# Moving the hand-placed SBUF area so that matmul operands and the weight ring start at the same place modulo 2048 bytes

## The chip, the cores and the metric

The program runs on one core of one Trainium2 chip. The metric is the device time of one execution in microseconds; lower is better. Three runs of the kernel before took 3888.85, 3893.64 and 3898.47 us, median 3893.64 us.

## What is computed

A stack of three transformer layers over one sequence of 512 tokens of width 1024, all in float32:

```python
for i in range(2):                                    # first block
    h = h + (mixer_ab if i == 0 else mixer_c)(rmsnorm(h))          # attention and recurrence
    h = h + conv_glu_ffn(rmsnorm(h))                               # 1024 -> 5632 -> 1024
    h = h + sigmoid(rmsnorm(h) @ ple_gate) * (p[i] @ ple_proj)
# second block: one layer
h = h + merged(diff_attention, chunk_attention)(rmsnorm(h)) @ w_out
h = h + peer(rmsnorm(h))     # routing picks 16 of 16384 single-neuron experts for each of 8 heads
return rmsnorm(h)
```

`peer` is computed densely: `gelu(xn @ u.T)` for all 16384 experts, times a routing matrix, times `v`. With the dense layers this makes one stream of 272 weight slots of 1 MB each.

## The kernel before

**Precision.** Every large product is made from operands that are split in two float32r parts, high and low. `split_product` (the matmul is line 189) issues three matmuls for one 128 x 128 x 512 product: high by high, low by high, high by low. Each is a weight load of 128 x 128 elements (512 bytes of each partition) and a stream of up to 512 moving columns (2048 bytes of each partition).

**The weight stream.** SyncE loads slot after slot (16 tiles of 128 x 128) into `weights_raw` (two places of 8 KB of each partition). GpSimd makes the high part with one TENSOR_SCALAR (line 2593) and the low part with one TENSOR_TENSOR (line 2595) in `weights_split`, the ring: two places of 16 KB, of which the first 8 KB are the high part and the next 8 KB the low part. TensorE waits for a place (`weights_ready`), uses it for 48 matmuls, and frees it for GpSimd. The hand-over, the order of the stages and all waits are written out by hand, and nothing in them depends on an address.

**Who is moving and who is loaded.** In most products a ring tile is loaded as weights and an operand of the hand-placed area moves (rows `banks<-memory,weights_split`). In the products "by token" and in the second half of the expert layer it is the other way round: 128-token slices of the operand are loaded and the ring moves (rows `banks<-weights_split,memory`).

**Where things lie.** In each partition, 16,512 bytes are taken by the runtime's scratch and four small constants; then come `residual` (16 KB, from byte 16,512), `weights_raw` (16 KB), `weights_split` (32 KB, from byte 49,280), `constants` (6,180 bytes, from 82,048), `columns` (2,912 bytes, from 88,256). The hand-placed area begins at the next multiple of 256, byte 91,392. Within it `Common` (line 498) takes 14 KB for four work tiles, `rstd` and the embedding, and two vectors of 128 bytes; then X_AT (32 KB), B_AT (56 KB) and HN_AT (32 KB) follow, in which every stage places its own buffers with `take` (line 235), rounded up to 128 bytes. Modulo 2048 this gives: residual, raw weights and ring tiles of index 0 at 128; the common tiles at 1280; the buffers that start at X_AT, B_AT and HN_AT at 1536. Modulo 256 the ring is at 128 and the area at 0. The tiles within a slot step by 512 bytes, the 512-column tiles of an operand by 2048.

**Lines that matter.** 189 split matmuls; 2593 and 2595 GpSimd's split; 443, 446 (ScalarE) and 452, 459 (VectorE) the norm's per-tile work, from `residual` into the area; 611 and 776 VectorE additions into `residual` and 677 one into a PSUM bank; 2213 a float32 matmul of one-hot rows and columns (`rows`, `cols`, both in the area, 512 bytes apart inside a tile and both tiles at the same place modulo 2048); 2240 float32 matmuls that load `residual` and move the identity of `constants`; 2361, 2367, 2483 the expert layer's gating; 2414 its activation; 2436 and 2439 the loads of routing and hidden values into the area; 1459 copies of 383 columns into rows that lie 1532 bytes apart.

Of the kernel before, what the change touches and what calls it, by code (L numbers as in the profile page):

```python
# [40 lines left out]
P = 128  # L41
TOKENS = 512
BLOCKS = TOKENS // P
# [41 lines left out]
CONST_AT, CONST_N = offsets(CONST_WIDTHS)  # L85
COLUMN_AT, COLUMN_N = offsets(COLUMN_WIDTHS)
# [90 lines left out]


KB = 1024
LINE = 128  # L180
X_AT = 14 * KB + 2 * LINE
B_AT = X_AT + 32 * KB
HN_AT = B_AT + 56 * KB


def split_product(k, out, left, right, start, stop):
# [9 lines left out]
class Core:  # L196


    def __init__(self, nc, ctx, dram):
        self.nc, self.ctx, self.dram = nc, ctx, dram  # L200
        self.period = None
        self.h = self.sbuf("residual", [P, D_TILES * TOKENS])
        self.raw = self.sbuf("weights_raw", [P, RING * SLOT])
        self.ring = ctx.enter_context(nc.sbuf_tensor("weights_split", [P, RING * 2 * SLOT], F32R))
        self.consts = self.sbuf("constants", [P, CONST_N])
        self.columns = self.sbuf("columns", [P, COLUMN_N])
        self.banks = ctx.enter_context(nc.psum_tensor("banks", [P, 8, 512], F32))
        self.arena = (nc.sbuf_base + 2 * LINE - 1) // (2 * LINE) * (2 * LINE)
        self.raw_in = [self.sem(f"weights_raw_in_{i}") for i in range(RING)]
        self.high_made = self.sem("weights_high_made")  # L210
        self.weights_ready = [self.sem(f"weights_split_{i}") for i in range(RING)]
        self.weights_used = [self.sem(f"weights_used_{i}") for i in range(RING)]
        self.meetings = self.sem("meetings")
        self.inputs_in = self.sem("inputs_in")
        self.held = self.sem("held")
        self.filled = self.sem("dense_filled")
        self.freed = {"vector": self.sem("dense_freed_vector"), "scalar": self.sem("dense_freed_scalar")}
        self.x_high, self.x_low, self.squared, self.summed, self.inverted = (
            self.sem(s) for s in ("operand_high", "operand_low", "squared", "squares_summed", "norm_inverted"))
        self.fills, self.frees, self.users, self.next_bank = 0, {"vector": 0, "scalar": 0}, {}, 0  # L220
        self.counts, self.kept = {}, {}
        self.tiles = 0
        self.pointer, self.named = 0, 0

    def sbuf(self, name, shape):
        return self.ctx.enter_context(self.nc.sbuf_tensor(name, shape, F32))
# [10 lines left out]
    def take(self, columns, dtype=F32):  # L237

        self.named += 1
        at = self.arena + self.pointer  # L240
        self.pointer += (4 * columns + LINE - 1) // LINE * LINE
        return self.nc.alloc_sbuf_tensor_at(f"memory_{self.named}", [P, columns], dtype, offset=at)[:, :]

    def take_split(self, tiles):
# [253 lines left out]
class Common:  # L498
# [3 lines left out]
    def __init__(self, k):  # L502
        self.work = [k.take(512) for _ in range(4)]
        self.rstd = k.take(512)
        self.embedding = k.take(PLE_TILES * 512)
        self.token_deviation, self.token_rstd = k.take(BLOCKS), k.take(BLOCKS)
        self.embedding_in = k.lasting("embedding_in")


# [654 lines left out]
def mixer_ab(k, common, hn, after_norm):  # L1164

    first = Norm(k, "mix0", hn, common, by_token=True)
    with k.scope(at=B_AT):
        heads = k.take(20 * 512)
        values = k.take(BLOCKS * 1024)
    with k.scope(at=X_AT):  # L1170
        out = k.take(BLOCKS * 1024)
    with k.scope(at=X_AT + 28 * KB):
        masks = k.take(8 * P)
# [6 lines left out]
    def evacuate(dve, n, bank):  # L1180
# [6 lines left out]
                           lambda part, b: cut(values, b * 1024 + part * 512, 512), meet=True)]  # L1187
    with k.scope(at=HN_AT):
        stages.append(stick_breaking(k, qa, ka, values, 1024, out, X_AT + 16 * KB))
    keep, decay = heads[:, 0:2048], heads[:, 2048:4096]  # L1190
# [300 lines left out]
def mixer_c(k, common, normed, after_norm):  # L1491
    with k.scope(at=B_AT):
# [3 lines left out]
        out = k.take(BLOCKS * 1024)  # L1496
    with k.scope(at=X_AT):
        table = k.take(SW_HEADS * 256)
# [114 lines left out]
def branches(k, common, normed, after_norm):  # L1613
# [22 lines left out]
        merged_high = k.take(8 * 512, F32R)  # L1636
    with k.scope(at=low_at):
        merged = Operand(k, merged_high, 8, k.take(8 * 512, F32R))
    with k.scope(at=HN_AT + 32 * KB):
        columns = Columns(k, 67)  # L1640
    even, odd = common.work[0:3], [common.work[3], odd_buffer]
    turned = [cut(common.embedding, n * 512, 512) for n in range(2)] + [third_turned]
# [876 lines left out]
def program(nc, dram):  # L2519
    ctx = ExitStack()  # L2520
    with ctx:
        k = Core(nc, ctx, dram)

        with k.scope(at=0):
            common = Common(k)
        assert k.arena + B_AT + 88 * KB <= nc.sbuf_usable_end
        with k.scope(at=X_AT):
            x = k.take(2 * D_TILES * TOKENS, F32R)
        with k.scope(at=HN_AT):
            hn = k.take(2 * D_TILES * TOKENS, F32R)  # L2530
        ffn_norm = [Norm(k, f"ffn{i}", x, common) for i in range(2)]
        ple_norm = [Norm(k, f"ple{i}", x, common) for i in range(2)]
        mix1_norm = Norm(k, "mix1", hn, common, by_token=True)
        norm1 = Norm(k, "norm1", hn, common, by_token=True)
        norm2 = Norm(k, "norm2", x, common)

        def layer(i):
            with k.scope(at=B_AT):
                stages = [load_embedding(k, i, common)] + feed_forward(k, i, common, ffn_norm[i], ple_norm[i])
            with k.scope(at=B_AT):  # L2540
                return stages + [layer_embedding(k, i, common, ple_norm[i], norm1 if i else mix1_norm)]

        def fresh(make):
            with k.scope(at=0):
                return make(k)

        stages = k.plan([
            lambda: [load_inputs(k)], lambda: fresh(bias_tables),
            lambda: mixer_ab(k, common, hn, ffn_norm[0]), lambda: layer(0),
            lambda: mixer_c(k, common, mix1_norm, ffn_norm[1]), lambda: layer(1),  # L2550
            lambda: branches(k, common, norm1, norm2), lambda: expert_layer(k, common, norm2)])

        def run(eng, which):

            met = 0
            for stage in stages:
                part = {"tensor": stage.tensor, "vector": stage.vector, "scalar": stage.scalar}[which]
                if part:
                    part(eng)
                if stage.meet:  # L2560
                    eng.drain().then_inc(k.meetings, 1)
                    met += 1
                    eng.wait_ge(k.meetings, 3 * met)

        block = ctx.enter_context(nc.Block())

        @block.sync
        def _(sp):
            def load(place, slot, turn):
                if turn is not None:  # L2570
                    sp.wait_ge(k.weights_ready[place], turn)
                sp.dma_start(k.raw[:, place * SLOT:(place + 1) * SLOT],
                             dram["weights"][bass.ds(slot, 1)].rearrange("s p n -> (s p) n")
                             ).then_inc(k.raw_in[place], 16)
            for place in range(RING):
                load(place, place, None)
            with sp.Fori(1, k.slots // RING) as turn:
                for place in range(RING):
                    load(place, turn * RING + place, turn)
            for place in range(k.slots % RING):  # L2580
                load(place, k.slots - 1, k.slots // RING)

        @block.gpsimd
        def _(pool):
            def split(place, turn):

                raw = k.raw[:, place * SLOT:(place + 1) * SLOT]
                high = k.ring[:, place * 2 * SLOT:place * 2 * SLOT + SLOT]
                low = k.ring[:, place * 2 * SLOT + SLOT:(place + 1) * 2 * SLOT]
                pool.wait_ge(k.raw_in[place], turn * 16 + 16)  # L2590
                pool.wait_ge(k.weights_used[place], turn + 1)
                k.hold(pool)
                k.nc.gpsimd.tensor_scalar(high, raw, 1.0, 1.0, ALU.mult, ALU.mult).then_inc(k.high_made, 1)  # L2593
                pool.wait_ge(k.high_made, turn * RING + (place + 1))
                k.nc.gpsimd.tensor_tensor(low, raw, high.bitcast(F32), ALU.subtract).then_inc(k.weights_ready[place], 1)  # L2595
            with pool.Fori(0, k.slots // RING) as turn:
                for place in range(RING):
                    split(place, turn)
            for place in range(k.slots % RING):
                split(place, k.slots // RING)  # L2600

        @block.tensor
        def _(pe):
            for place in range(RING - 1):
                pe.sem_inc(k.weights_used[place], 1)
            run(pe, "tensor")

        @block.vector
        def _(dve):
            run(dve, "vector")  # L2610

        @block.scalar
        def _(act):
            run(act, "scalar")
    return k
# [110 lines left out]
```

## Time and profile before

| what | value |
|---|---|
| median of three runs | 3893.64 us (3888.85 to 3898.47) |
| profiled execution, own time | 3901.22 us |
| its span, first to last instruction | 3899.4 us |
| mean granted TensorE clock | 0.949 |
| TensorE busy | 3655.5 us (94%) |
| VectorE, ScalarE, GpSimd busy | 2079.0, 923.7, 1818.9 us |
| DMA | 441.04 MB, mean 113 GB/s |

The span is read by engine and then by the chain that ended last, in which each piece is either work or a wait. Busy time of TensorE counts a matmul from its start to its modelled end, so consecutive matmuls overlap; the pace of TensorE is the length of an unbroken piece of the chain divided by the number of its matmuls.

### The profile page before, as it was taken

The numbers are of one execution on the slowest core, as the hardware profiler recorded it, in microseconds if no ns is written. First come the engines' busy times: TensorE is split into PE (matmuls) and PEld (weight loads), VectorE is DVE, ScalarE is ACT, GpSimd is POOL, SyncE is SP. The second block draws the span as 40 slices with busy tenths as digits, with TensorE's granted clock in tenths as the row PEclk, the third lists the DMA queues.
The fourth block names the chain that finished last, engine by engine and source line by source line (L and its number), as shares of the span: only waits on it lengthen the run. The fifth ranks groups of instructions, "written<-read, shape, count | busy, mean of one in ns | idle before, by whom it ended". The sixth has DMA issues, their size and how long they took to land.

```text
span 3899.4 us, 44573 instructions
## 1 busy us (share of the span) xinstructions
PE 3655.5 (94%) x16472; PEld 2938.4 (75%) x16472; DVE 2079.0 (53%) x3529; ACT 923.7 (24%) x1682; POOL 1818.9 (47%) x548
## 2 busy tenths in 40 slices
PE   6975599999879999999999999999999999999999
PEld 4864578887556788878677878888888878888887
DVE  3014664416454544261662288885555447777775
ACT  1054322202144222020453111113333311111111
POOL 2510055655300565555333556564444456666664
PEclk9987799999855999999999999999999999999999
DMA  4200022222200222222111223334444465555552
GB/s 176 93 26 0 1 103 92 93 97 87 76 1 6 96 88 97 97 92 84 57 60 65 97 93 134 143 133 157 183 189 167 178 232 191 198 175 198 188 183 97
DMA packets 133929, 441.04 MB, mean 113 GB/s; under 512 B 7040, under 2 KB 76800, under 8 KB 96640
## 3 DMA queue, kind: packets, MB, share of 16 engines
q1 hardware_dynamic: 39168, 285.23, 20.5%
q10 hardware_dynamic: 94592, 153.41, 10.9%
q8 instruction: 124, 2.03, 0.2%
q14 instruction: 45, 0.37, 0.0%
HBM read 363.65 MB, written 74.96 MB: 112 GB/s over the span
## 4 chain that ended last, share of the span: by engine, by line
PE 79%; DVE 5%; ACT 2%; issue 1%; ACTq 1%; DVEq 0%; DMA 0%
PE banks L189 70%; PE banks L2213 3%; PE banks L1250 1%; DVE memory L459 1%; PE banks L1274 1%; DVE memory L1893 1%; DVE memory L1525 1%; PE banks L1264 1%; PE banks L1780 1%; PE banks L1742 1%; ACT memory L2010 1%; ACTq L2439 0%; DVE memory L452 0%; PE banks L1759 0%; PE banks L812 0%
## 5 line engine op out<-in xcount | busy, mean ns | idle before, releaser
L189 PE MATMUL banks<-memory,weights_split 128*128 128x512 f32 x9456 | 2272.0, 399 | 52.9 <-DVE memory L452 40.5
L189 PEld LDWEIGHTS banks<-memory,weights_split 128*128 128x128 f32 x9456 | 1780.3, 190 | 489.3 <-DVE memory L452 46.8
L2593 POOL TENSOR_SCALAR weights_split<-weights_raw 128x2048 fp32r<-128x2048 f32 x272 | 535.9, 1970 | 2033.3 <-issue 1186.4
L2595 POOL TENSOR_TENSOR weights_split<-weights_raw,weights_split 128x2048 fp32r<-128x2048 f32 x272 | 1282.8, 4716 | 22.7
L189 PE MATMUL banks<-weights_split,memory 128*128 128x512 f32 (+1 forms) x3648 | 837.7, 392 | 0.0
L189 PEld LDWEIGHTS banks<-weights_split,memory 128*128 128x128 f32 x3648 | 680.5, 188 | 156.5
L2361 DVE TENSOR_TENSOR memory<-memory,memory 128x512 f32<-128x512 f32 x128 | 361.1, 2822 | 52.7 <-DMA memory<-hidden 46.2
L2346 DVE TENSOR_SCALAR memory<-banks,memory 128x128 f32<-128x128 f32 x512 | 174.1, 401 | 218.7 <-PE banks L2213 212.8
L2367 DVE TENSOR_TENSOR memory<-memory,memory 128x512 fp32r<-128x512 f32 x128 | 179.7, 1404 | 175.2 <-ACT memory L2483 175.2
L2483 ACT ACTIVATE memory<-memory 128x512 fp32r<-128x512 f32 x128 | 80.8, 632 | 618.0 <-PE banks L189 613.7
L2414 ACT ACTIVATE memory<-banks 128x512 f32<-128x512 f32 x128 | 76.5, 598 | 572.9 <-PE banks L189 553.0
L656 DVE TENSOR_TENSOR banks<-banks,memory 128x512 f32<-128x512 f32 x88 | 61.3, 699 | 243.3 <-PE banks L189 243.2
L611 DVE TENSOR_TENSOR residual<-banks,residual 128x512 f32<-128x512 f32 x32 | 22.1, 690 | 231.1 <-PE banks L189 231.1
L2426 ACT ACTIVATE memory<-banks 128x512 f32<-128x512 f32 x128 | 131.4, 1133 | 21.2 <-PE banks L2213 21.2
L704 ACT ACTIVATE memory<-banks,columns 128x512 f32<-128x512 f32 x88 | 68.4, 780 | 274.8 <-DVE banks L656 274.8
L2213 PEld LDWEIGHTS banks<-memory,memory 128*128 128x128 f32 x1024 | 124.1, 191 | 5.8
L2213 PE MATMUL banks<-memory,memory 128*128 128x128 f32 x1024 | 124.5, 275 | 0.0
L443 ACT ACTIVATE memory<-residual,columns 128x512 fp32r<-128x512 f32 x64 | 46.1, 720 | 330.4 <-DVE residual L611 281.6
L459 DVE TENSOR_TENSOR memory<-memory,memory 128x512 f32<-128x512 f32 x56 | 120.6, 2153 | 0.0
L452 DVE SCALAR_TENSOR_TENSOR memory<-residual,columns,memory 128x512 fp32r<-128x512 f32 x64 | 96.6, 1509 | 26.3 <-ACT memory L443 26.3
L1114 PE MATMUL banks<-memory,memory 128*128 128x128 f32 x256 | 47.6, 352 | 49.0 <-DVE memory L1039 47.5
L1250 PE MATMUL banks<-memory,memory 64*128 64x256 f32 (+1 forms) x128 | 66.8, 643 | 26.1 <-DVE memory L1574 26.1
(238 smaller groups left out, 2554.3 us busy)
## 6 DMA issues: line engine op xcount, KB each, us to landing
weights_raw<-in_weights SPq DMA_DIRECT2D x272, 1024.0 KB, 4.8
hidden<-memory ACTq DMA_DIRECT2D x64, 512.0 KB, 2.6
routing<-memory ACTq DMA_DIRECT2D x16, 2048.0 KB, 6.2
memory<-routing ACTq DMA_DIRECT2D x32, 1024.0 KB, 6.7
memory<-hidden ACTq DMA_DIRECT2D x32, 1024.0 KB, 9.0
window_rows<-memory ACTq DMA_DIRECT2D x4, 766.0 KB, 5.7
chunk_rows<-memory ACTq DMA_DIRECT2D x1, 2556.0 KB, 8.9
residual<-in_x ACTq DMA_DIRECT2D x1, 2048.0 KB, 14.3
```

The lines of the kernel that those rows point to most:

```text
L189: last = k.nc.tensor.matmul(out, left[a], right[b], start=start and n == 0, stop=stop and n == 2, skip_group_check=True)
L452: v.scalar_tensor_tensor(out=self.out.low(n), in0=cut(k.h, n * 512, 512), scalar=k.column(self.gain, n), in1=self.out.high(n).bitcast(F32) ...
L459: v.tensor_tensor(self.total, self.squares[0] if n == 1 else self.total, self.squares[n % 2], ALU.add).then_inc(k.summed, 1)
L1250: k.nc.tensor.matmul(k.banks[:, u % 3, 0:blocks * P], query, key, start=True, stop=True).then_inc(scored, 1)
L2213: last = mm(score_banks[g % DEPTH].memory[:, s], rows[g % DEPTH][:, s], cols[g % DEPTH][:, s], start=True, stop=True, skip_group_check=True)
L2346: last = v.tensor_scalar(rows[g % DEPTH][:, t * P:(t + 1) * P], iota, cut(turned, at, 1), cut(turned, 2 * TOKENS + at, 1), ALU.is_equal, A ...
L2361: v.tensor_tensor(gated[e % 2].rearrange("p (c t) -> p c t", c=TOKENS // PORTION), cut(kept[place], e % GROUP * 512, 512).rearrange("p (c ...
L2367: v.tensor_tensor(operand.low(e % 4), gated[e % 2], operand.high(e % 4).bitcast(F32), ALU.subtract).then_inc(ready, 1)
L2426: a.activation(by_token[:, at:at + BATCH, :], score_banks[g % DEPTH].memory.rearrange("p (t n) -> p t n", t=BATCH), ACT.Copy).then_inc(mat ...
L2483: a.activation(operand.high(e % 4), gated[e % 2], ACT.Copy).then_inc(high_made, 1)
L2593: k.nc.gpsimd.tensor_scalar(high, raw, 1.0, 1.0, ALU.mult, ALU.mult).then_inc(k.high_made, 1)
L2595: k.nc.gpsimd.tensor_tensor(low, raw, high.bitcast(F32), ALU.subtract).then_inc(k.weights_ready[place], 1)
```

## The change

The area begins directly at the end of the ring, byte 82,048, and X_AT becomes 14 KB instead of 14 KB + 256 bytes. So the common tiles and the buffers at X_AT, B_AT and HN_AT are all at 128 modulo 2048, the same as the ring and the residual. `constants` and `columns` are placed 512 bytes after the end of HN_AT's 32 KB, the two small vectors of `Common` and the 67 columns of `branches` directly behind those 32 KB. `take` rounds to 32 bytes instead of 128; this moves only what follows a size that is not a multiple of 128 bytes (in `bias_tables` the chunk rows start 160 bytes lower relative to the area, and short vectors lie closer together). No instruction, wait or transfer is added or taken away.

```diff
-LINE = 128
-X_AT = 14 * KB + 2 * LINE
+X_AT = 14 * KB
 B_AT = X_AT + 32 * KB
 HN_AT = B_AT + 56 * KB
+SMALL_AT = HN_AT + 32 * KB
...
         self.ring = ctx.enter_context(nc.sbuf_tensor("weights_split", [P, RING * 2 * SLOT], F32R))
-        self.consts = self.sbuf("constants", [P, CONST_N])
-        self.columns = self.sbuf("columns", [P, COLUMN_N])
+        self.arena = nc.sbuf_base
+        assert self.arena % 32 == 0
+        self.pointer, self.named = SMALL_AT + 512, 0
+        self.consts, self.columns = self.take(CONST_N), self.take(COLUMN_N)
+        assert self.arena + self.pointer <= nc.sbuf_usable_end
         self.banks = ctx.enter_context(nc.psum_tensor("banks", [P, 8, 512], F32))
-        self.arena = (nc.sbuf_base + 2 * LINE - 1) // (2 * LINE) * (2 * LINE)
...
-        self.pointer += (4 * columns + LINE - 1) // LINE * LINE
+        self.pointer += (4 * columns + 31) // 32 * 32
...
-        self.token_deviation, self.token_rstd = k.take(BLOCKS), k.take(BLOCKS)
+        with k.scope(at=SMALL_AT):
+            self.token_deviation, self.token_rstd = k.take(BLOCKS), k.take(BLOCKS)
...
-    with k.scope(at=HN_AT + 32 * KB):
+    with k.scope(at=SMALL_AT + 64):
         columns = Columns(k, 67)
```

## Rows read from the trace of the kernel before

**Rows 1.** The page: span, busy time by engine (share) and instructions.
```profile
span 3899.4 us, 44573 instructions
PE 3655.5 (94%) x16472; PEld 2938.4 (75%) x16472; DVE 2079.0 (53%) x3529; ACT 923.7 (24%) x1682; POOL 1818.9 (47%) x548
```

**Rows 2.** The chain that ended last, by engine: shares of the span.
```profile
PE 79%; DVE 5%; ACT 2%; issue 1%; ACTq 1%; DVEq 0%; DMA 0%
PE banks L189 70%; PE banks L2213 3%; PE banks L1250 1%; DVE memory L459 1%; PE banks L1274 1%; DVE memory L1893 1%; DVE memory L1525 1%; PE banks L1264 1%; PE banks L1780 1%; PE banks L1742 1%; ACT memory L2010 1%; ACTq L2439 0%; DVE memory L452 0%; PE banks L1759 0%; PE banks L812 0%
```

**Rows 3.** Pieces of the chain, operand moving: start us, us, what.
```profile
538.55 356.94 PE banks L189 x1536
1320.32 356.94 PE banks L189 x1536
2326.56 78.28 PE banks L189 x336
2647.25 5.58 PE banks L189 x24
3111.35 5.58 PE banks L189 x24
```

**Rows 4.** The same, ring moving.
```profile
3176.30 709.01 PE banks L189 x3051
```

**Rows 5.** Busy us of each engine in two such stretches, clock, DMA.
```profile
1320.00:1677.00 357.00, 357.00 (x1537) 289.35 (x1536) 138.56 (x195) 69.14 (x104) 209.68 (x64) 1.00 0.27 94
3180.00:3880.00 700.00, 700.00 (x3014) 567.49 (x3013) 522.21 (x247) 78.38 (x124) 428.63 (x125) 1.00 0.53 178
```

**Rows 6.** Pieces of the chain, float32 matmuls of 128 columns.
```profile
3116.93 1.78 PE banks L2213 x16
3169.15 7.14 PE banks L2240 x64
```

**Rows 7.** Groups by line and form: count | busy us, mean ns | idle before.
```profile
L189 PE MATMUL banks<-memory,weights_split 128*128 128x512 f32 x9456 | 2272.0, 399 | 52.9 <-DVE memory L452 40.5 <-DVEq L2561 7.6 <-ACT memory L2414 4.0
L189 PE MATMUL banks<-weights_split,memory 128*128 128x512 f32 x3552 | 826.2, 395 | 0.0
L2595 POOL TENSOR_TENSOR weights_split<-weights_raw,weights_split 128x2048 fp32r<-128x2048 f32 x272 | 1282.8, 4716 | 22.7
L459 DVE TENSOR_TENSOR memory<-memory,memory 128x512 f32<-128x512 f32 x56 | 120.6, 2153 | 0.0
L611 DVE TENSOR_TENSOR residual<-banks,residual 128x512 f32<-128x512 f32 x32 | 22.1, 690 | 231.1 <-PE banks L189 231.1
L677 DVE TENSOR_TENSOR banks<-banks,memory 128x512 f32<-128x512 f32 x44 | 30.3, 690 | 0.1
L446 ACT ACTIVATE memory<-residual 128x512 f32<-128x512 f32 x64 | 39.6, 619 | 20.0 <-DVE memory L459 19.9
L2483 ACT ACTIVATE memory<-memory 128x512 fp32r<-128x512 f32 x128 | 80.8, 632 | 618.0 <-PE banks L189 613.7 <-DMA hidden<-memory 2.7 <-DVE memory L2361 1.7
```

**Rows 8.** One line's instructions: ns min/median/max.
```profile
L1459 DVE COPY memory<-banks x16: 543/556/559, 25.8 to 42.1; 128x383 f32<-128x383 f32 x16
```

**Rows 9.** Pieces of the chain in the gated part before a norm.
```profile
939.28 5.09 DVE memory L459
955.62 0.68 DVE memory L459
961.59 5.04 DVE memory L459
```

**Rows 10.** The chain at ScalarE's loads, start us, us, what.
```profile
3142.11 1.10 ACTq L2436
3143.24 2.87 ACTq L2439
3146.14 0.51 ACTq L2436
3146.68 7.13 ACTq L2439
3153.84 2.07 ACTq L2436
3155.94 5.05 ACTq L2439
```

**Rows 11.** DMA queues (packets, MB, share of 16 engines) and issues (KB, us to landing).
```profile
q1 hardware_dynamic: 39168, 285.23, 20.5%
q10 hardware_dynamic: 94592, 153.41, 10.9%
weights_raw<-in_weights SPq DMA_DIRECT2D x272, 1024.0 KB, 4.8
memory<-hidden ACTq DMA_DIRECT2D x32, 1024.0 KB, 9.0
```

More of the change, by code:

```diff
@@ L222, in __init__ @@
         self.tiles = 0
-        self.pointer, self.named = 0, 0
+        self.pointer = 0
     def sbuf(self, name, shape):
@@ L2525, in program @@
             common = Common(k)
-        assert k.arena + B_AT + 88 * KB <= nc.sbuf_usable_end
         with k.scope(at=X_AT):
```

## The prediction

> **What bounds the kernel now.** I read the page's busy line first. It shows TensorE busy for 94% of the span and no other engine above 53% [rows 1]. The reader is to see there that one engine fills the span, but not yet at what pace. The chain that ended last is the second view: TensorE is 79% of it, and one line, the split matmul of line 189, is 70%; VectorE is 5%, ScalarE 2% [rows 2]. 70% of 3899.4 us is some 2740 us (the long pieces of rows 3 and 4 hold more than half of it). The third view is the chain's long pieces, because a piece of unbroken matmuls divided by their number is the pace. The two feed-forward layers each have a piece of 356.94 us with 1536 matmuls, 232.4 ns each; the routing part has 78.28 us for 336, 233.0 ns; the batches beside the routing matrix have 5.58 us for 24, 232.5 ns [rows 3]; the last stage has 709.01 us for 3051, 232.4 ns [rows 4]. So 2740 us of the chain are about 2740 / 0.2324 = 11,790 matmuls, and each nanosecond on the pace is worth 11.8 us, which is 0.3% of the time. A stream of 512 columns at the 2.4 GHz that rows 5 grant (clock 1.00) needs 512 / 2.4 = 213.3 ns. The excess is 19.1 ns a matmul, 225 us on the chain. That excess is the only place in which a change of addresses alone could move much.
>
> **The change part by part.** Nothing is added or removed, so the sum is made of pace changes, each multiplied by its count.
>
> *TensorE, operand against ring.* Before, an operand buffer lies at 1536 and the first ring tile at 128 modulo 2048, a distance of 1408; the ring's tiles step by 512, so the distance takes four values, all of them 128 modulo 256. After, the distances are 0, 512, 1024 and 1536. The question is whether the pace depends on the distance. What the rows show: (a) the pieces of rows 3 run through all four distances, with high and low parts, and the pace of a whole piece is 232.4 ns; 24 matmuls that cover only eight tiles take 5.58 us at 2647 us and 5.58 us at 3111 us; (b) when ring and operand change roles, so that the moving stream starts at 128 instead of 1536 and the weight load at the operand, the pace is 232.4 ns again [rows 4]; (c) it is the same with GpSimd busy 209.68 of 357 us and DMA at 94 GB/s as with GpSimd and VectorE busy 428.63 and 522.21 of 700 us and DMA at 178 GB/s [rows 5]. A pace that keeps its fourth digit under all of that looks like a fixed cost of the float32r stream and not like collisions in memory. What the rows don't show is a float32r pair whose distance is 0 modulo 256. The nearest are float32 matmuls: rows and columns of line 2213 lie at distances 0 and 512, residual and identity of line 2240 at multiples of 512; they take 1.78 / 16 = 111.3 ns and 7.14 / 64 = 111.6 ns [rows 6]. A float32 matmul of 128 columns stands as two instructions; if each streams its columns twice, that is 106.7 ns and an excess of 4.6 to 4.9 ns (the two streams are my reading). Equal places don't hurt them. Bounds for the 512-column pair: below, the excess falls to those 4.9 ns, a gain of 14.2 ns; above, the excess doubles, a loss of 19.1 ns. I take 0, since the rows nearest in kind (float32r, four distances, both roles) show no dependence at all. Term: 0, bounds -167 and +225 us.
>
> A rule weighed against this row: the Trainium skill, "TensorE: Matmul & The Clock Gate", section "Back-to-back issue gap", gives N / 2.4 + 2.5 ns for one matmul after another, which is 215.8 ns at 512 columns, and its "Step-by-step" section says that weight loads and the moving stream have separate read ports, so that the one takes no bandwidth from the other. The trace's 232.4 ns disagrees with the first. If the missing 16.6 ns were a collision that the new layout removes, the sum would be 11,790 x 16.6 ns = 196 us less, an estimate from that page; by the second sentence there is no collision to remove, and the sum stays.
>
> *VectorE and ScalarE.* Their operands move from 0 to 128 modulo 256. The trace has both places side by side. An addition that reads and writes `residual` (at 128) takes 690 ns, one that reads the area (at 0) 690 ns; a square from `residual` into the area takes 619 ns, a copy inside the area 632 ns [rows 7]. Sixteen copies into rows that lie 1532 bytes apart, at sixteen different places, take 543 to 559 ns [rows 8]. The largest of these spreads is 3%; on the chain's 7% of VectorE and ScalarE (273 us) it would be 8 us either way. Most of that spread isn't ordered by place, so I take 0, bounds -8 and +8.
>
> *GpSimd.* `weights_raw` and the ring stay where they are, so 4716 ns for the low part [rows 7] stays; it has slack anyway: one slot costs TensorE 48 x 0.2324 = 11.2 us. Term 0.
>
> *DMA.* Buffers of the area start at 128 modulo 256 instead of 0. The raw weights have always been at 128 and the 16 engines give them 285.23 MB / (0.205 x 3899.4 us x 16) = 22.3 GB/s of engine time; the other queue, mostly to and from the area at 0, has 153.41 / (0.109 x 3899.4 x 16) = 22.6 [rows 11]. A place at 128 costs nothing that these rows show. Where transfers are on the chain they are short: before the last stage ScalarE issues six loads for 18.7 us while the hidden activations wait [rows 10]; later ones are hidden behind 709 us of matmuls. The nearest difference is 22.3 against 22.6, 1.3%, 0.2 us of 18.7; the upper bound is that every 512-byte run costs half as much again, 9.4 us. I take 0, bounds 0 and +9.
>
> The Trainium skill, "DMA: Bandwidth & Descriptors", section "How a descriptor splits into AXI transactions", speaks against the change: a run that doesn't start at a multiple of 256 bytes needs a partly used first transaction. Applied to the 512-byte runs of the routing loads that is three instead of two, hence an estimate of +9 us at most; the rates of the two queues above don't bear it out.
>
> *Small vectors and constants.* They are read as scalars or weight tiles of full width, and lose nothing by lying elsewhere. The chunk rows' new place touches one DVE pair and one transfer in the first 40 us. Term 0.
>
> *Phase.* A VectorE instruction with two SBUF inputs takes 0.68 us, or about 5 us when it meets GpSimd's 4.7 us one; on the chain before the norms the same addition stands with 5.09, 0.68 and 5.04 us [rows 9], and its mean over 56 is 2153 ns [rows 7]. A shift in time of a microsecond redraws this lottery. Two draws more or less are 2 x 4.3 = 9 us.
>
> **Sum.** 3901.2 us of the profiled execution + 0 = 3901.2. The profiled execution was 7.6 us above the median of the runs (3893.64), and the changed kernel is timed in runs like those: 3894 us. Bounds of the small terms together are some -17 to +26; as they don't fall together I take 3880 to 3908 as this case's own range. About 0.3%, 12 us, is what a measurement of this kernel can tell from no change.
>
> **The rivals.** *A, the excess was a collision between weight load and stream, and equal places lift it.* For: 19.1 ns are unexplained, and float32 pairs at equal places have only 4.9. Against: no trace of a dependence in rows 3 to 5, and float32 pairs differ in kind. Full relief 14.2 ns x 11,790 = 167 us: 3727 us; it counts as faster from 1 ns on. GpSimd would not bound it: a slot would take 48 x 0.218 = 10.5 us. *B, the other sign: at equal places the load and the stream of line 189 want the same part of memory at the same time, which at 128 modulo 256 they never did.* For: this distance is new to float32r. Against: lines 2213 and 2240 run at equal places without loss. Place: every matmul of rows 3 and 4; price, if each pays once more the 4.9 ns of rows 6, 58 us: 3952 us; decides from 1 ns. *C, the phase lottery* falls by more than two draws: 12 to 20 us, 3878 or 3910. *D, DMA at 128* costs its bound of 9 us and a few more in the first 60 us: 3907. *E, the layout is not what it says*: the operands might not land at the ring's place. The addresses follow from the sizes (82,048 is 128 modulo 2048), so I give this nothing of its own; its time would be that of no change.
>
> **How the numbers follow.** No change 0.64; A 0.15; B 0.12; C beyond 12 us 0.06, half on each side; D beyond 12 us 0.03. Faster 0.15 + 0.03 = 0.18; slower 0.12 + 0.03 + 0.03 = 0.18; same 0.64. The range runs from 3850 to 3955: it holds the first case, C, D, the 4.9 ns form of B and the first 3.7 ns of A, and leaves out full relief and a doubled excess.
>
> **What would show it.** The pieces of line 189 at the same counts: 356.94 us for 1536 if I am right, 335 if A, 364 or more if B. The rows of lines 611, 446 and 2483 at 690, 619 and 632 ns; the six loads at 18.7 us for D; the sum of line 459 for C. A changed pace in only one of the two roles (ring loaded, ring moving) would show that the start of one stream matters and not the distance. The prediction is wrong if the pace moves by 1 ns.

## The result and the profile after

The changed kernel takes 3826.93 us (median of four runs, 3825.32 to 3827.49), the kernel before 3896.05 us beside it (four runs, 3888.85 to 3903.56). The ratio is 0.9822, 95% interval 0.9802 to 0.9841: 1.8% or some 69 us faster. I had forecast no change. The profiled execution took 3827.37 us, its span is 3825.5 us, 73.9 us less than the span before.

The page after, first lines and the chain by engine and line (shares of the span):

```profile
span 3825.5 us, 44573 instructions
PE 3576.0 (93%) x16472; PEld 2922.0 (76%) x16472; DVE 2079.5 (54%) x3529; ACT 923.6 (24%) x1682; POOL 1829.5 (48%) x548
...
PE 79%; DVE 5%; ACT 2%; issue 1%; ACTq 1%; DVEq 0%; DMA 0%
```

The same instructions run, VectorE and ScalarE are busy to the microsecond as before, and the shares of the chain are those of [rows 2]. The page alone can't tell where the time went. The chain's long pieces can (start us, us, what; lines behind 189 moved down by two or three):

```profile
531.01 348.22 PE banks L189 x1536
1297.60 348.22 PE banks L189 x1536
2285.68 76.39 PE banks L189 x336
2598.57 5.47 PE banks L189 x24
3119.76 691.59 PE banks L189 x3051
```

Each answers to a piece of [rows 3, 4] with the same count: 348.22 against 356.94, 76.39 against 78.28, 5.47 against 5.58, 691.59 against 709.01 us. The pace is 226.7 ns instead of 232.4, in both roles, with little or much other work beside it. The last stage alone gives 17.4 us. Added up over all its pieces, the chain holds 11,733 matmuls of line 189 in both traces, 2741.6 us before and 2676.9 after: 64.7 of the 73.9 us.

The single matmuls show more than the mean does. In the same 100 us of the last stage, before and then after (ns min/median/max from the start of one to its modelled end):

```profile
L189 PE MATMUL banks<-weights_split,memory x432: 390/393/404, 3399.7 to 3499.8; 128*128 128x512 f32 x144
L189 PE MATMUL banks<-weights_split,memory x443: 389/389/389, 3399.8 to 3500.0; 128*128 128x512 f32 x148
```

Before, each matmul had its own price; from start to start they were 228 to 241 ns apart, with a mean of 232.4. After, they are 226 or 227 ns apart, each one.

The rest of the change moved little. Groups of the kernel after (count | busy us, mean ns of one | idle before):

```profile
L614 DVE TENSOR_TENSOR residual<-banks,residual 128x512 f32<-128x512 f32 x32 | 22.1, 690 | 223.2 <-PE banks L189 223.2
L448 ACT ACTIVATE memory<-residual 128x512 f32<-128x512 f32 x64 | 39.6, 619 | 20.4 <-DVE memory L461 20.3
L2486 ACT ACTIVATE memory<-memory 128x512 fp32r<-128x512 f32 x128 | 80.8, 632 | 601.0 <-PE banks L189 596.6 <-DMA hidden<-memory 2.7 <-DVE memory L2364 1.7
L461 DVE TENSOR_TENSOR memory<-memory,memory 128x512 f32<-128x512 f32 x56 | 123.8, 2211 | 0.0
```

690, 619 and 632 ns are those of [rows 7] to the nanosecond, although the operands now lie 128 bytes off. Line 461, the lottery between VectorE and GpSimd, has 3.2 us more busy time than its 120.6 before, but not on the chain. Its pieces of some 5 us there are eight (at 882, 923, 944, 1282, 1649, 1688, 1710 and 2235 us), as they were before (at 898, 939, 962, 1305, 1680, 1721, 1743 and 2275 us), and all its pieces on the chain sum to 46.2 us in both traces.

The stretch of ScalarE's loads on the chain (start us, us, what) also answers to rows shown before, [rows 10]; it sums to 19.2 us against 18.7 (the two hardware queues are busy for 20.8% and 11.1% of the shorter span, which is 22.4 and 22.6 GB/s of engine time against 22.3 and 22.6):

```profile
3084.81 1.26 ACTq L2439
3086.10 2.70 ACTq L2442
3088.83 1.03 ACTq L2439
3089.89 7.91 ACTq L2442
3097.82 0.50 ACTq L2439
3098.36 5.81 ACTq L2442
```

### The profile page after: what moved, and what is told of

Same layout as the page of the kernel before. It is cut to its first block, busy times and chain, and to the rows that moved or that the text cites. A ratio compares the mean times of both kernels' runs of the same rounds, so it can differ in the third digit from the quotient of the medians.

```text
span 3825.5 us, 44573 instructions
## 1 busy us (share of the span) xinstructions
PE 3576.0 (93%) x16472; PEld 2922.0 (76%) x16472; DVE 2079.5 (54%) x3529; ACT 923.6 (24%) x1682; POOL 1829.5 (48%) x548
## 3 DMA queue, kind: packets, MB, share of 16 engines
q1 hardware_dynamic: 39168, 285.23, 20.8%
q10 hardware_dynamic: 94592, 153.41, 11.1%
## 4 chain that ended last, share of the span: by engine, by line
PE 79%; DVE 5%; ACT 2%; issue 1%; ACTq 1%; DVEq 0%; DMA 0%
PE banks L189 70%; PE banks L2216 3%; PE banks L1253 1%; DVE memory L461 1%; PE banks L1277 1%; DVE memory L1896 1%; DVE memory L1528 1%; PE banks L1267 1%; PE banks L1783 1%; ACT memory L2013 1%; PE banks L1745 1%; ACTq L2442 0%; DVE memory L454 0%; PE banks L1762 0%; DVE memory L1893 0%
## 5 line engine op out<-in xcount | busy, mean ns | idle before, releaser
L189 PE MATMUL banks<-memory,weights_split 128*128 128x512 f32 x9456 | 2221.4, 394 | 55.6 <-DVE memory L454 40.8
L2597 POOL TENSOR_TENSOR weights_split<-weights_raw,weights_split 128x2048 fp32r<-128x2048 f32 x272 | 1286.3, 4729 | 22.7
L189 PE MATMUL banks<-weights_split,memory 128*128 128x512 f32 (+1 forms) x3648 | 817.4, 386 | 0.0
L707 ACT ACTIVATE memory<-banks,memory 128x512 f32<-128x512 f32 x88 | 68.5, 781 | 263.4 <-DVE banks L659 263.4
L445 ACT ACTIVATE memory<-residual,memory 128x512 fp32r<-128x512 f32 x64 | 46.2, 721 | 320.5 <-DVE residual L614 274.1
L454 DVE SCALAR_TENSOR_TENSOR memory<-residual,memory,memory 128x512 fp32r<-128x512 f32 x64 | 96.1, 1502 | 26.1 <-ACT memory L445 26.1
```

The lines of the kernel that those rows point to most:

```text
L189: last = k.nc.tensor.matmul(out, left[a], right[b], start=start and n == 0, stop=stop and n == 2, skip_group_check=True)
L454: v.scalar_tensor_tensor(out=self.out.low(n), in0=cut(k.h, n * 512, 512), scalar=k.column(self.gain, n), in1=self.out.high(n).bitcast(F32) ...
```

## The experiments

Four variants of the two kernels move whole parts by some bytes. Three small programs measure the disputed cost alone: their TensorE part is a list of lines, each one loop of 48 matmuls that loads tiles at a place w and moves columns from a place m, both modulo 2048, tile after tile 2048 bytes apart. A pair (w, m) below is such a line; its distance is m - w, and "modulo 256" means what is left of it after whole multiples of 256. The piece of the chain divided by 48 is that line's pace. Where a pace is given "from start to start", it is the mean time between the starts of the line's matmuls from the fifth on, which leaves out what the line before left behind. The small programs leave out the whole computation of the reference. Three explanations compete, by number in the expectations: the distance between load and stream (1), the place of one of the two by itself (2), and something else that the change moved (3).

### m1: places, TensorE alone

```diff
+            for i in range(48): last = mm(out(i), load(0, i), move(128, i), **flags)
...
+            for i in range(48): last = mm(out(i), load(128, i), move(128, i), **flags)
```

> A measurement of the disputed cost by itself: after filling 48 KB with float32r values nothing runs but TensorE. 42 lines of 48 float32r matmuls each; a line keeps the place of its weight load (w) and of its moving columns (m) modulo 2048, the area begins at a multiple of 2048. It computes nothing of the reference. Theory 1 (distance): the pace is 226.7 ns where m - w is a multiple of 256 and 232.4 ns where it is 128 modulo 256, whatever w is: (0,0), (128,128), (64,64), (1536,128)+0 like pairs tell. Theory 2 (absolute place): the pace follows whether the moving columns (or the load) start at 128 modulo 256, so (128,128) and (0,0) differ. Theory 3 (neither; something else of the change did it): all lines at one pace. For 16, 32 and 64 bytes no theory has a number from the two traces; if the distance counts, they tell from which step on.

Its chain, start us, us, what. Lines 2555, 2560, 2563, 2565 and 2566 load at 0 and move from 0, 128, 256, 512 and 640; 2576 and 2577 load at 128 and move from 128 and 192; 2578 loads at 128 and moves from 256; 2584 and 2585 load at 32 and move from 32 and 160:

```profile
44.13 10.88 PE banks L2555 x48
...
99.52 11.20 PE banks L2560 x48
...
133.16 10.92 PE banks L2563 x48
...
155.27 10.89 PE banks L2565 x48
166.17 11.19 PE banks L2566 x48
...
276.56 10.90 PE banks L2576 x48
287.46 11.00 PE banks L2577 x48
298.47 11.16 PE banks L2578 x48
...
365.06 10.91 PE banks L2584 x48
375.97 11.19 PE banks L2585 x48
```

10.88 to 10.92 us is 226.7 to 227.5 ns, 11.19 is 233.1, 11.16 is 232.5. So nothing of the kernel is needed but TensorE, and the place of neither stream counts by itself: (0, 0), (128, 128) and (32, 32) are all fast, (0, 128) and (32, 160) slow. All thirteen lines whose distance m - w was a multiple of 256 (-256 to 1792) took 10.88 to 10.93 us, also those at w = 64 and w = 256. The lines at 128 modulo 256 took 11.16 to 11.20. This is theory 1, with one small addition: shifting load and stream together isn't quite without effect on the slow pace. From start to start (0, 128) takes 233.4 ns, (128, 256) and (64, 192) take 232.4; the fast pace stays within 0.6 ns. In between it is not a smooth curve: from start to start the paces at 16, 32, 64, 96, 160 and 192 bytes are 231.6, 233.4, 228.9, 233.5, 234.2 and 233.4 ns. A fast and a slow line, 2555 and 2560, differ in their single matmuls as the two kernels do:

```profile
L2555 PE MATMUL banks<-big x48: 389/389/389, 44.0 to 54.6; 128*128 128x512 f32 x48
L2560 PE MATMUL banks<-big x48: 392/394/398, 99.4 to 110.3; 128*128 128x512 f32 x48
```

### e1: only the area of the kernel before, 128 bytes further

```diff
-        self.arena = (nc.sbuf_base + 2 * LINE - 1) // (2 * LINE) * (2 * LINE)
+        self.arena = (nc.sbuf_base + 2 * LINE - 1) // (2 * LINE) * (2 * LINE) + 128
```

> The kernel before with its area 128 bytes further, so that operands and ring are 1536 and multiples of 512 apart in place of 1408; rounding, constants and vectors as before. Theory 1 (distance modulo 256): pace 226.7 ns, 348.2 us for 1536 matmuls, about 3827 us. Theory 2 (the area at 128 modulo 256): the same. Theory 3 (what else the change moved: constants, vectors, rounding to 32): 232.4 ns and about 3894 us.

Measured: 3829.2 us (four runs), ratio to the kernel before 0.982 (0.9804 to 0.9837). From its chain:

```profile
534.68 348.22 PE banks L189 x1536
...
3126.10 691.59 PE banks L189 x3051
```

The whole gain is there, with `constants`, `columns` and the rounding to 128 bytes as they were, and with a distance of 1536 instead of 0 modulo 2048. One line does it, and modulo 256 is enough.

### e2: the changed kernel, its area 128 bytes further

```diff
-        self.arena = nc.sbuf_base
+        self.arena = nc.sbuf_base + 128
```

> The changed kernel with its whole area, constants included, 128 bytes further: distance 128, area at 256 modulo 2048. Theories 1 and 2: 232.4 ns, 356.9 us for 1536, about 3894 us. Theory 3: stays at 226.7 ns and 3827 us.

Measured: 3897.44 us (ten runs), ratio 0.9999 (0.9989 to 1.0008): the gain is gone, and with it every part above some 4 us (the interval) that the constants, the vectors and the tighter rounding could have had. From its chain:

```profile
535.42 356.94 PE banks L189 x1536
...
2323.06 78.59 PE banks L189 x336
...
3172.70 709.01 PE banks L189 x3051
```

### e3: the changed kernel, everything 128 bytes further

```diff
+        self.pad = self.sbuf("pad", [P, 32])
         self.h = self.sbuf("residual", [P, D_TILES * TOKENS])
```

> The changed kernel with 128 unused bytes ahead of residual, raw weights, ring and area: the distances stay 0, but ring and area are now both at 0 modulo 256. Theory 1 (distance): 226.7 ns, about 3827 us. Theory 2 (absolute place): 232.4 ns, about 3894 us.

Measured: 3834.17 us, one run, pieces as fast as in the changed kernel:

```profile
535.60 348.22 PE banks L189 x1536
...
3126.66 691.59 PE banks L189 x3051
```

Ring and area now start at multiples of 256. Theory 2 calls that slow, since the area at 0 modulo 256 was slow before. It is fast, so the distance is the cause.

### m2: steps, lengths, turns

```diff
+            for i in range(48): last = mm(out(i), load(0, i), move(240, i), **flags)
...
+            for i in range(48): last = mm(out(i, 384), load(0, i), move(128, i, 384), **flags)
```

> The same measurement with other lines; it computes nothing of the reference. Steps: with the distance as cause and 226.7 ns at 0, distances of 4 to 12 bytes should stay at or near 226.7 if a collision needs another piece of memory than 16 bytes, and 208 to 252 (just below a multiple of 256) tell whether it matters who is ahead: 233 if only the equal start helps, about 227 to 229 if the stream may be a little behind. Lengths 128 to 512 columns at distances 0 and 128: theory 4, at distance 0 the stream runs at full rate and 13.3 ns stay for each matmul, so the pace is N / 2.4 + 13.3 (360 where N is 384 is 173.3, 128 is 66.7 unless the weight load of some 110 ns is longer); rival, the cost grows with N. Alternating pairs: the load that runs beside a stream is that of the next matmul. With (w, m) = (0, 0), (128, 128) in turn every matmul has its own load at its place and the next one's 128 away; with (0, 128), (128, 0) the other way round. If the next load collides, the first is slow (233) and the second fast (227); if its own, the reverse. Loads of 64 columns: if the load makes the excess, half a load halves it.

The places are finer than I expected. Paces from start to start for w = 0:

| m | 0 | 4 | 8 | 12 | 48 | 80 | 112 | 144 | 176 | 208 | 224 | 240 | 248 | 252 |
|---|---|---|---|---|---|---|---|---|---|---|---|---|---|---|
| ns | 226.7 | 235.7 | 233.3 | 229.9 | 233.4 | 231.2 | 231.3 | 233.4 | 231.1 | 234.7 | 233.4 | 226.7 | 234.1 | 229.9 |

The pieces of its chain for m = 0, 4 and 240 (start us, us, what) and for 384 columns at distances 0 and 128 (lines 2579 and 2580):

```profile
42.92 10.88 PE banks L2555 x48
53.80 11.32 PE banks L2556 x48
...
165.48 10.89 PE banks L2566 x48
...
267.71 8.32 PE banks L2579 x48
276.04 8.45 PE banks L2580 x48
```

Four bytes cost 9 ns, so "stays near 226.7 up to 12 bytes" was wrong. Sixteen bytes behind (240, and w = 16 with m = 0) is as good as equal, sixteen ahead costs 4.9 ns: it matters who is ahead. No place was faster than 226.65.

Paces by the number of columns, from start to start:

| columns | 128 | 192 | 256 | 320 | 384 | 448 | 512 |
|---|---|---|---|---|---|---|---|
| N / 2.4, ns | 53.3 | 80.0 | 106.7 | 133.3 | 160.0 | 186.7 | 213.3 |
| distance 0 | 111.7 | 111.7 | 119.9 | 146.7 | 173.4 | 202.7 | 227.2 |
| distance 128 | 111.7 | 111.6 | 118.6 | 146.7 | 176.1 | 203.9 | 233.4 |

At distance 0 the pace is N / 2.4 + 13.3 ns for 256, 320, 384 and 512 columns, as theory 4 said (448 has 2.7 ns more, which stays open; 512 stands with 227.2 behind a slow line, and with 226.7 in the first table). At 128 and 192 columns the pace is 111.7 ns at either distance; that the loads set it there is the likely reading, which no line tests. The distance costs only from 384 columns on, and at 256 columns distance 0 is even 1.2 ns worse. Turns (0, 0), (128, 128) took 228.4 ns and turns (0, 128), (128, 0) 230.0: neither the own nor the next load alone. Loads of 64 columns took 229.9 at distance 0 and 229.4 at 128: with half a load the distance all but stops counting, and the 13.3 ns don't halve; they grow to 16.6.

### e4: a distance that tells the two roles apart

```diff
-        self.arena = (nc.sbuf_base + 2 * LINE - 1) // (2 * LINE) * (2 * LINE)
+        self.arena = (nc.sbuf_base + 2 * LINE - 1) // (2 * LINE) * (2 * LINE) + 192
```

> The kernel before with its area 192 bytes further: operands 1600, that is 64 modulo 256, ahead of the ring where the operand moves; where the ring moves it is 64 behind (192). From the lines (0,64) and (0,192) of the first measurement, 228.9 and 233.4 ns: theory 1 expects 351.5 us for 1536 matmuls with the operand moving and about 712 us for the 3051 with the ring moving, so the two roles part; in all (8,740 x -3.5 + 3,050 x +1.0) ns = 28 us less than before, 3868 us. Theory 2 (absolute places): both roles at one pace, 3827 or 3894 us.

Measured: 3868.97 us (four runs), ratio 0.9928 (0.9912 to 0.9945), and the pieces part:

```profile
534.34 351.60 PE banks L189 x1536
...
3139.61 711.91 PE banks L189 x3051
```

351.60 where 351.5 was expected, 711.91 where 712 was, and 29 us less than the kernel before beside it (3898.33, seven runs), where 28 was expected. The small program's lines for 64 and 192 carry over to the whole kernel, and a distance of 64 in one role is 192 in the other. The line for 128 carries over less exactly: where the ring moves, the kernel before has load and stream as in (1536, 128), which takes 233.4 ns in m1 and 232.4 in the kernel. The kernel steps its loads by 512 bytes and m1 by 2048; whether that makes the 1 ns was not tested.

### m3: types, turns, other engines beside it

```diff
+            for i in range(48): last = mm(out(i), load(0, i).bitcast(F32), move(128, i).bitcast(F32), **flags)
...
+            for i in range(48): last = mm(out(i), half(load(0, i), P), half(move(128, i), 512), **flags)
...
+            pe.sem_inc(done, 1)
+            for i in range(48): last = mm(out(i), load(0, i), move(128, i), **flags)
```

> The third measurement of that kind; it computes nothing of the reference. Types: float32 matmuls of 512 columns at distances 0, 64, 128, 192 and bfloat16 ones of 512 and 128 columns. If the distance is a matter of float32r's single pass of four bytes a column, float32 pairs (two instructions, each streaming twice as long) stay at one pace near 429 ns an instruction whatever the distance, as line 2213 and 2240 of the kernel do, and bfloat16 stays at one pace; rival: the collision hits every type, float32 at 128 loses 6.7 ns or more too. Turns: load fixed at 0 with the stream at 0 and 128 in turn should give the mean of the two, 230.0, if each matmul's price depends on one load and one stream alone; in twos, (0, 0) twice and (128, 128) twice, the next load is elsewhere for every second matmul: 230.0 if the next load decides, 226.7 if its own, something else if neither is the whole rule. 256 apart in turn: 226.7, if only the place modulo 256 counts. The last four lines, beside GpSimd and VectorE at work: 226.7 and 233.4 as before, if the collision is inside TensorE's own reading; more than that at either, if other engines' accesses take part.

Its chain: 2570 and 2571 are float32r at distances 0 and 128, 2572 to 2575 float32 at 0, 64, 128 and 192, 2576 to 2579 bfloat16 at the same four, 2587 and 2588 float32r at 0 and 128 beside GpSimd and VectorE:

```profile
43.92 10.88 PE banks L2570 x48
54.80 11.19 PE banks L2571 x48
65.99 41.20 PE banks L2572 x96
107.19 41.20 PE banks L2573 x96
148.39 41.20 PE banks L2574 x96
189.59 41.20 PE banks L2575 x96
230.79 10.36 PE banks L2576 x48
241.15 10.36 PE banks L2577 x48
251.51 10.36 PE banks L2578 x48
261.87 10.36 PE banks L2579 x48
...
321.87 10.88 PE banks L2587 x48
332.75 11.19 PE banks L2588 x48
```

and its busy time in the stretch of those last lines, in which VectorE and GpSimd were at work for 44 and 25 of 46 us (span, then PE, PEld, DVE, POOL, clock, DMA share, GB/s):

```profile
320.00:366.00 46.00, 46.00 (x201) 37.25 (x199) 44.37 (x39) 24.61 (x12) 1.00 0.00 1
```

Float32 and bfloat16 of 512 columns have one pace at all four distances; float32r has its two paces with VectorE and GpSimd at work as without them. Of the turns, the load at 0 with the stream at 0 and 128 took 230.05 ns, the mean of the two; but (0, 0) twice and (128, 128) twice took 231.7, with starts 235 and 228 ns apart in turn, more than either theory gave, and a load that alternates between 0 and 128 under a stream at 0 took 232.3. 256 apart in turn: 226.7. So a price per pair of load and stream is not the whole rule; what went before counts too.

## Why the prediction was wrong

**The failed step** is "TensorE, operand against ring": "I take 0, since the rows nearest in kind (float32r, four distances, both roles) show no dependence at all". The term measured -64.7 us on the chain (11,733 matmuls, 5.7 ns on each in the unbroken pieces). That lies inside the bounds of -167 and +225 that I had set, and the range that I gave left it out. Three errors made the 0. First, the four distances of [rows 3], 1408 and steps of 512 from it, are one distance modulo 256; so are the two roles, since 128 and -128 are the same modulo 256. I had written this down ("all of them 128 modulo 256"; "what the rows don't show is a float32r pair whose distance is 0 modulo 256") and still counted the rows as evidence against a dependence. They could only show that bits 9 and 10 of the distance don't count. Second, "a pace that keeps its fourth digit" was a mean over hundreds of matmuls that differ. The trace before shows single matmuls of 390 to 404 ns; a fixed cost looks like the 389 of every matmul after. The view that shows it, one line's min/median/max, was there before the change, and it spoke against a fixed cost. Third, the float32 lines 2213 and 2240 were no substitute: float32 of 512 columns has one pace at all four distances tried (m3), and the two lines stream only 128 columns, at which float32r has no dependence either (111.7 ns at both distances, m2).

**Rival A** had the mechanism: equal places lift an excess of float32r. Its size was off, 14.2 ns where 5.7 came, because I took the 4.9 ns of a float32 instruction as the floor. The lowest that float32r showed at any place is 13.3 ns (m2). A chance of 0.15 for it was too little: the excess of 19.1 ns was unexplained, and where their operands lie was the one thing about these matmuls that the change altered. **Rival B** is refuted for 512 columns and true in small at 256: 119.9 against 118.6 ns, 96 matmuls in the kernel. One of my signs would have misled: I wrote that a change in only one of the two roles would show that the start of one stream matters and not the distance. e4 changes the two roles by different amounts (-3.5 and +1.0 ns), and the distance explains it, because it has a sign that turns with the roles.

**The other terms** held. VectorE and ScalarE 0, to the nanosecond in the lines named. GpSimd: its low part takes 4729 ns against 4716. DMA: 0.5 us on the six loads, of a bound of 9. Small vectors and constants 0: e1 leaves `constants` and `columns` in place and has the gain, e2 has them moved and has none. Phase: the lottery cost nothing on the chain.

The sum of the 73.9 us: 64.7 are line 189 on the chain. 3.0 are the net of the rest of the chain; the largest changes there are 16 matmuls of line 812 that no longer stand on it (-3.8 us), VectorE at line 833 (+1.9) and the loads (+0.5). 6.2 lie ahead of the point from which the chain can be followed (456.3 us before, 450.1 after). The long piece begins 7.5 us earlier than before. That start goes with the granted clock and not with the distance: up to the long piece TensorE stood at the lower of its two levels, 1.2 GHz, for 126.0 us before and for 112.3 after. In e1, e2, e3 and e4 it was 115.8, 119.2, 122.7 and 115.8 us, and their long pieces begin at 534.7, 535.4, 535.6 and 534.3 us, between the 531.0 after and the 538.6 before and in the same order, although e2 has the slow pace and e1 and e3 the fast one. So these microseconds are most likely a difference between executions. No run was made to test that.

**The rule weighed against the row.** m3 has 10.36 us for 48 bfloat16 matmuls, 215.8 ns each. That agrees with N / 2.4 + 2.5 ns for 512 columns in the Trainium skill, "TensorE: Matmul & The Clock Gate", section "Back-to-back issue gap". The same section gives that formula for a single matmul's gap, and about 131 ns at 512 columns for a stream with a load each; m3's stream has a load each and takes 215.8, so here the measurement decides. For float32r it decides too: 226.7 at best. The statement of the same page of the Trainium skill, in "Step-by-step", that a load takes no read bandwidth from the running matmul agrees with bfloat16 and float32 at all four distances, and not with float32r, where moving the load alone by 128 bytes changes the pace from 226.7 to 233.4 ns.

What stays open: what in the chip the load and the stream share ("collision" is a picture; the runs show a dependence on the distance), why 4 bytes cost more than 128, and how the previous pair enters. No version in these runs beats the changed kernel; e1 ties with it (ratios 0.9820 and 0.9822).

## What to carry to other kernels

When a row is used as evidence that something doesn't matter, write down which values of it the row covered, modulo whatever could count; rows that sample one class say nothing of the other. Look at the spread of single instructions before calling a mean a fixed cost. For long float32r matmuls place the weight tiles and the moving tiles so that their starts differ by a multiple of 256 bytes; here that is one added constant and 1.8%. Where an unexplained excess stands on 70% of the chain, a small program with one line of matmuls for each layout settles it in one run of 0.5 ms.

## What the runs showed of the hardware

- Float32r, 128 x 128 load, 512 columns at 2.4 GHz: 226.7 ns a matmul where m - w is a multiple of 256 (also 16 bytes less), 228.8 to 235.7 ns at the other distances tried, the last at 4 bytes. When load and stream move together, the fast pace keeps within 0.6 ns and the slow one at 128 within 1.1 (m1, m2, e3).
- At distance 0 a float32r matmul of 256, 320, 384 or 512 columns takes its columns at 2.4 GHz plus 13.3 ns; at 128 and 192 columns it takes 111.7 ns (m2). The distance costs nothing up to 320 columns and 2.7 ns at 384.
- Float32 (429.2 ns an instruction) and bfloat16 (215.8 ns) of 512 columns had one pace at distances 0, 64, 128 and 192 (m3).
- Operands 128 bytes off left VectorE and ScalarE at 690, 619 and 632 ns in the lines compared and the DMA queues at 22.4 and 22.6 GB/s of engine time; six loads on the chain took 19.2 us in place of 18.7.
- A float32r matmul at a fast distance takes 389 ns from start to modelled end, all but alike (388 to 390 in the changed kernel, e1 and e3); at a slow one single matmuls spread, 390 to 404 ns in the kernel before and e2, 392 to 398 in m1.
